# Two-block transformer kernel: closing norm in two token halves, second feed-forward norm with its root and tiles in PSUM, other banks for the first pairs of two stages

## Chip, cores, metric

One core of one Trainium2 chip. The metric is the device time of one execution in microseconds; three runs of the kernel before gave 1818.01, 1818.57 and 1822.48, median 1818.57.

## What is computed

Two transformer blocks over 512 tokens of width 1024, all in 32-bit floats, transposed (features on partitions, tokens on columns). The part that matters here:

```
x = x + rmsnorm(merged @ w_out[l], g_mix_post[l])        # out2, post2
h = rmsnorm(x, g_ffn_pre[l])                             # the norm of ffn2
gu = h @ w_ffn_in[l]                                     # ffn2, 44 units
f = (jax.nn.silu(gu[..., :D_FF_2]) * gu[..., D_FF_2:]) @ w_ffn_out[l]   # down2a, down2b
x = x + rmsnorm(f, g_ffn_post[l])                        # closing norm and store
```

with `rmsnorm(x, g) = x * rsqrt(mean(x * x) + eps) * g` over the features of a token. The first block has the same shape: out1, ffn1, down1a and down1b.

## The kernel before

**Weights.** All weight matrices are one stream of 278 units of 128 x 1024 (512 KB). A ring of three slots holds them: SP loads a unit into `w_raw` (L318), ScalarE rounds it to `w_hi` (L820, `feed`), GpSimd computes the rest `w_lo = w_raw - w_hi` (L335, `low_part`), and TensorE forms each product as three matmuls, hi x hi, hi x lo and lo x hi (`split_mm`, L378 to L380). A slot is filled again once `w_used` has counted the unit that was in it; `feed_after(t)` feeds unit t + 2. GpSimd's work is the ring, in the order of the units; `ring(0, FIRST["ffn2"] + AHEAD)` runs until two units of ffn2 are split, then come the seven sums of squares of ffn2's norm (L356), then the ring goes on.

**Stages.** Each stage multiplies a run of units with an activation tensor that is held as a hi and a lo part. `tiles_loop` runs out1, ffn1, out2 and ffn2: every unit gives 128 output features for 512 tokens, 24 matmuls of 512 columns in one PSUM bank, units alternating between banks 0 and 1. The first two units run together (`two_units`): k tile by k tile, as the lo parts of the input become ready, in banks 0 and 1. TensorE takes a bank with `acquire`, which waits for the reader's `bank_free`.

**Out2 to ffn2.** VectorE copies each unit of out2 to `o2` (L1773), ScalarE squares, VectorE sums (L1343), TensorE multiplies the sum with a matrix of ones (L514, `norm`; fp32, it stands in the trace as two records), ScalarE makes the root by Ln and Exp (L849, L851) in `tmp[3]`. Then `post` on VectorE, for each of eight tiles: scale by root and gain (L1793), add to `hT` (L1798), and the low part `u_lo` for ffn2 (L1372, `raw_low`); ScalarE squares (L845) and makes `u_hi` (L855); GpSimd sums the squares (L356). Ffn2 begins on the unnormed `u_hi`, `u_lo`; its root is applied to the outputs. Before the last k tile of the first two units TensorE runs the ones matmul. In `ffn_dve` VectorE handles a pair of units: gate times root (L1643), sigmoid on ScalarE (L1160), two products, the other unit (L1651), and the split of the result into `a_hi` (L1654) and `a_lo` (L1655). The gate's read frees bank 0 (L1644), the other bank 1.

**Down and close.** `down2a` and `down2b` accumulate eleven units each into four banks (2 to 5, then 6, 7, 0, 1); the last unit goes bank by bank. VectorE copies each bank to `o3` (L1809), the squares are summed, one ones matmul, one root, then `post` again: eight scales of 512 columns on VectorE (L1793), adds to `hT` alternately on VectorE (L1798) and GpSimd (L361), and eight stores of 256 KB by SP (L326). The file's helpers `step` and `wait_ge` order the engines by semaphores; nothing else plans the work.

Of the kernel before, what the change touches and what calls it, by code (L numbers as in the profile page):

```python
# [26 lines left out]
P = 128  # L27
# [87 lines left out]
def build(nc, stream, xT, memT, vecs, tabs, relb, outT):  # L115
    with ExitStack() as ctx, ExitStack() as work:
# [110 lines left out]
        sticks = [tmp[0], tmp[1], at("stick2", [P, T], F32, mv_at), at("stick3", [P, T], F32, mv_at + 2 * K)]  # L227
        zero_l = ar("zero_l", [P, P], BF16, 72)
# [7 lines left out]
        ps = ctx.enter_context(nc.psum_tensor("ps", [P, 8, T], F32))  # L236

# [28 lines left out]
        PER_NORM = {"sq": KT, "add": KT - 1, "ms": 1, "rs": 1}  # L266

        def of_norm(name, kind, value):

            if kind in PER_NORM:  # L270
                before_it = NORMS.index(name) * PER_NORM[kind]
            else:
                before_it = (SCALED if kind == "u" else SPLITS).index(name) * KT
            return named("norm_" + kind), before_it + value


# [16 lines left out]


# [7 lines left out]
        def _(sp):  # L302
# [24 lines left out]
            sp.wait_ge(out_done, 16 * KT)  # L327
# [3 lines left out]
        def _(pool):  # L331
# [18 lines left out]
            ring(0, FIRST["ffn2"] + AHEAD)  # L350

            for k in range(1, KT):
# [3 lines left out]
                pool.tensor_tensor(tmp[2][:, :], tmp[2][:, :], tmp[k % 2][:, :], ALU.add).then_inc(named("norm_add"), 1)  # L356
            ring(FIRST["ffn2"] + AHEAD, UNITS)

            for k in range(1, KT, 2):
                pool.wait_ge(named("y_out_scaled"), k + 1)  # L360
                pool.tensor_tensor(hT[:, k], hT[:, k], tmp[4 + k % 2][:, :], ALU.add).then_inc(named("y_odd"), 1)  # L361
# [3 lines left out]
        def _(pe):  # L365
# [26 lines left out]
            def two_units(t, xh, xl, n, ready, before_last=None):  # L392

                pe.wait_ge(lo_ready, t + 2)
                acquire(0)
                acquire(1)
                for k in range(KT):
                    if k == KT - 1 and before_last:
                        before_last()
                    pe.wait_ge(*(of_norm(*ready, k + 1) if isinstance(ready, tuple) else (ready, k + 1)))  # L400
                    c = slice(k * P, k * P + P)
                    for j in range(2):
                        slot = (t + j) % R
                        m = split_mm(ps[:, j, 0:n], w_hi[:, slot, c], w_lo[:, slot, c], xh[:, k], xl[:, k],
# [53 lines left out]
            def tiles_loop(name, n, xh, xl, ready, before_last=None):  # L458

                u, turn = FIRST[name], 2 * R  # L460
                two_units(u, xh, xl, T, ready, before_last)
                for j in range(2, turn):
                    tile_unit(u + j, (u + j) % R, j % 2, xh, xl)
# [58 lines left out]
            def softmax_attention(name, steps, head_q, head_k, keys, values, extra, out_of, opens, ready, between,  # L522
# [6 lines left out]
                for g in range(turns + 2):  # L529
                    if g < turns:  # L530

                        if g >= 1:
                            pe.wait_ge(named(name + scored), 2 * g)
# [5 lines left out]
                        for e in range(2):  # L539
# [5 lines left out]
                            m.then_inc(named(name + "_s"), 1)  # L545
                    if g >= 2:
# [5 lines left out]
                        pe.wait_ge(named(name + "_pt"), s + 2)  # L552
                        nb = keys[steps[s][1]] // P
                        two_heads = steps[s][0] != steps[s + 1][0]
                        for e, kb in sorted(product(range(2), range(nb)), key=lambda x: x[::-1] if two_heads else x):
# [4 lines left out]
                            if kb == nb - 1:  # L560
                                m.then_inc(named(name + "_av"), 1)
# [4 lines left out]
                    if 1 <= g <= turns:  # L566
                        if g == 1:
                            settle([4, 5])
                        for e in range(2):
                            s = 2 * (g - 1) + e  # L570

                            pe.wait_ge(named(name + "_pn"), s + 1)
# [3 lines left out]
                            m.then_inc(named(name + "_t"), 1)  # L576
# [89 lines left out]
            for j in range(8):  # L666
                if j == 1:
                    pe.wait_ge(named("moba_y"), 4)
                yh, yl = (yb_hi, yb_lo) if j % 2 == 0 else (ya_hi, ya_lo)
                up_unit(u + j, (u + j) % R, yh, yl, 2 * (j % 2))  # L670
            tiles_loop("out1", 8, m1_hi, m1_lo, ready=named("m1_lo_done"))
            tiles_loop("ffn1", 44, u_hi, u_lo, ("n_ffn", "lo"), lambda: norm("n_ffn", T))
# [113 lines left out]
            pe.wait_ge(named("dsa_y"), 4)  # L786
            pe.wait_ge(named("mem_y"), 4)
# [8 lines left out]
            tiles_loop("out2", 8, m2_hi, m2_lo, ready=named("m2_lo_done"))  # L796
            norm("n_post2", T)
            tiles_loop("ffn2", 44, u_hi, u_lo, ("n_ffn2", "lo"), lambda: norm("n_ffn2", T))
            down("down2a", [2, 3, 4, 5], named("ffn2_a"))
            down("down2b", [6, 7, 0, 1])  # L800
# [1173 lines left out]
```

## Time and profile before

| what | value |
|---|---|
| three runs | 1818.01, 1818.57, 1822.48 us |
| profiled execution, its own time | 1820.88 us |
| its span, first to last instruction | 1819.1 us |
| TensorE busy | 1726.2 us, 95% |
| VectorE, ScalarE, GpSimd busy | 869.7, 625.1, 704.9 us |
| mean granted TensorE clock | 0.987 of full speed |
| memory traffic | 162.21 MB moved, mean 89 GB/s |

The profile follows one execution. A busy share is an average over stages; what a change in a stage is worth is read from the waits of that stage. Times in a row of a timeline are counted from the start of the span, and a bracket at its end tells how long the engine had stood idle before it and which instruction released it.

### The profile page before, as it was taken

What the parts mean: (1) busy time and instruction counts of PE and PEld (TensorE: products, weight loads), DVE (VectorE), ACT (ScalarE), POOL (GpSimd) and SP (SyncE); (2) the same over time, 40 slices, a digit from 0 to 9 for tenths busy, and PEclk for the clock granted to TensorE, in tenths of its full rate; (3) what the DMA queues carried; (4) which work ended last, traced back from release to release, by engine and by line L of the source; (5) the groups of instructions that cost most, each with busy time, mean ns of one, the idle gap of its engine ahead of it and who ended that gap; (6) DMA issues with size and microseconds to landing.
All of it is one profiled execution on the core that took longest, in us unless ns stands there. A gap on an engine that the chain in (4) does not pass through costs nothing.

```text
span 1819.1 us, 23230 instructions
## 1 busy us (share of the span) xinstructions
PE 1726.2 (95%) x7880; PEld 1356.0 (75%) x7888; DVE 869.7 (48%) x1341; ACT 625.1 (34%) x997; POOL 704.9 (39%) x293
## 2 busy tenths in 40 slices
PE   5999999999999999998899899999999699999995
PEld 4888666777888887886578655668888488888884
DVE  6603665573655552035497756541332755555003
ACT  5233444434222223234424444453222422222221
POOL 2544222244544444444243111224444444444442
PEclk9999999999999999999999999999999899999998
DMA  4434311223322232234122111112332132232321
GB/s 154 160 130 117 103 58 47 69 72 115 113 94 92 94 103 93 93 104 151 61 93 74 43 36 35 59 45 95 94 102 93 36 115 92 92 103 94 103 93 46
DMA packets 46189, 162.21 MB, mean 89 GB/s; under 512 B 5564, under 2 KB 5692, under 8 KB 45864
## 3 DMA queue, kind: packets, MB, share of 16 engines
q1 hardware_dynamic: 42576, 151.16, 25.4%
q10 hardware_dynamic: 3544, 10.13, 1.7%
q8 instruction: 43, 0.70, 0.2%
q14 instruction: 26, 0.21, 0.0%
HBM read 156.91 MB, written 4.76 MB: 89 GB/s over the span
## 4 chain that ended last, share of the span: by engine, by line
PE 53%; issue 29%; POOL 10%; DVE 6%; ACT 2%; POOLq 0%; DVEq 0%; ACTq 0%
PE ps L378 16%; PE ps L380 16%; PE ps L379 16%; POOL w_lo L335 10%; PE ps L537 1%; PE ps L558 1%; DVE tmp L1343 1%; DVE tmp L1793 1%; PE ps L574 1%; PE ps L749 1%; DVE sum L1763 1%; PE ps L705 1%; DVE hT L1798 1%; PE ps L771 0%; PE ps L514 0%
## 5 line engine op out<-in xcount | busy, mean ns | idle before, releaser
L335 POOL TENSOR_TENSOR w_lo<-w_raw,w_hi 128x1024 fp32r<-128x1024 f32 x278 | 686.7, 2472 | 1068.4 <-ACT w_hi L820 1068.3
L378 PE MATMUL ps<-u_hi,w_hi 128*128 128x512 f32 x1392 | 565.1, 406 | 37.5 <-DVE u_lo L1355 11.6
L380 PE MATMUL ps<-u_hi,w_lo 128*128 128x512 f32 x1392 | 546.3, 392 | 0.0
L379 PE MATMUL ps<-u_lo,w_hi 128*128 128x512 f32 x1392 | 545.8, 392 | 0.0
L820 ACT ACTIVATE w_hi<-w_raw 128x1024 fp32r<-128x1024 f32 x278 | 292.7, 1055 | 425.5 <-PE ps L380 384.9
L378 PEld LDWEIGHTS ps<-u_hi,w_hi 128*128 128x128 f32 x1392 | 263.1, 189 | 117.0 <-issue 54.2
L380 PEld LDWEIGHTS ps<-u_hi,w_lo 128*128 128x128 f32 x1392 | 263.2, 189 | 56.4
L379 PEld LDWEIGHTS ps<-u_lo,w_hi 128*128 128x128 f32 x1392 | 263.6, 189 | 52.9 <-issue 2.4
L378 PE MATMUL ps<-a_hi,w_hi 128*128 (+1 forms) x352 | 137.2, 390 | 0.3 <-POOL w_lo L335 0.3
L380 PE MATMUL ps<-a_hi,w_lo 128*128 (+1 forms) x352 | 137.0, 389 | 0.0
L379 PE MATMUL ps<-a_lo,w_hi 128*128 (+1 forms) x352 | 137.0, 389 | 0.0
L1655 DVE TENSOR_TENSOR a_lo<-tmp,a_hi 128x512 f32 (+1 forms) x44 | 115.8, 2632 | 5.2
L1160 ACT ACTIVATE tmp<-tmp 128x512 f32<-128x512 f32 x44 | 27.8, 632 | 222.0 <-DVEq L1645 221.9
L1651 DVE TENSOR_TENSOR tmp<-ps,tmp 128x512 f32<-128x512 f32 x44 | 30.4, 692 | 100.5 <-PE ps L380 100.2
L378 PEld LDWEIGHTS ps<-a_hi,w_hi 128*128 128x128 f32 x352 | 66.1, 188 | 14.4 <-issue 0.8
L379 PEld LDWEIGHTS ps<-a_lo,w_hi 128*128 128x128 f32 x352 | 66.1, 188 | 13.8
L380 PEld LDWEIGHTS ps<-a_hi,w_lo 128*128 128x128 f32 x352 | 66.1, 188 | 13.7
L1643 DVE TENSOR_TENSOR tmp<-ps,tmp 128x512 f32<-128x512 f32 x44 | 30.4, 692 | 62.3 <-PE ps L380 49.5
L1809 DVE COPY o<-ps 128x512 f32<-128x512 f32 x8 | 5.5, 688 | 106.8 <-PE ps L380 106.8
L1613 DVE TENSOR_TENSOR tmp<-ps,tmp 128x512 f32<-128x512 f32 x16 | 11.1, 692 | 91.1 <-PE ps L380 90.0
L1679 DVE TENSOR_TENSOR hT<-ps,hT 128x512 f32<-128x512 f32 x8 | 5.5, 688 | 98.1 <-PE ps L380 98.1
L378 PE MATMUL ps<-m_hi,w_hi 128*128 128x512 f32 x128 | 50.0, 391 | 1.4 <-DVEq L1587 0.9
(279 smaller groups left out, 2160.7 us busy)
## 6 DMA issues: line engine op xcount, KB each, us to landing
w_raw<-stream SPq DMA_DIRECT2D x278, 512.0 KB, 3.5
g_rep<-g_one ACTq DMA_DIRECT2D x1, 2560.0 KB, 15.2
hT<-xT SPq DMA_DIRECT2D x4, 512.0 KB, 5.2
spread<-m_rows ACTq DMA_DIRECT2D x4, 512.0 KB, 4.6
tmp<-tmp ACTq DMA_DIRECT2D x32, 64.0 KB, 3.6
bias<-g_rep ACTq DMA_DIRECT2D x1, 2048.0 KB, 7.9
outT<-hT SPq DMA_DIRECT2D x8, 256.0 KB, 2.0
mem_in<-memT ACTq DMA_DIRECT2D x1, 1024.0 KB, 4.8
```

Source lines behind the costliest of these rows:

```text
L335: pool.tensor_tensor(w_lo[:, slot], w_raw[:, slot], w_hi[:, slot].bitcast(F32), ALU.subtract)\
L378: pe.matmul(out, wh, xh, start=start, stop=False)
L379: pe.matmul(out, wh, xl, start=False, stop=False)
L380: return pe.matmul(out, wl, xh, start=False, stop=stop)
L537: both.append(pe.matmul(ps[:, 2 + e, 0:keys[t]], head_q(h, t), head_k(h, keys[t]), start=True, stop=not extra(t)))
L558: m = pe.matmul(ps[p0:p1, b, t * P:t * P + P], values(h, kb), prT[e][:, kb * P:kb * P + P], start=kb == 0, stop=kb == nb - 1)
L574: m = pe.transpose(ps[:, 4 + e, kb * P:kb * P + P], pr[s % 4][:, kb * P:kb * P + P], ident)
L820: act.activation(w_hi[:, slot], w_raw[:, slot], ACT.Copy).then_inc(hi_ready, 1)
L1160: act.activation(tmp[0][:, :], tmp[1][:, :], ACT.Sigmoid).then_inc(named(name + "_e"), 1)
L1643: step(dve.tensor_tensor(tmp[1][:, :], ps[:, 0, :], tmp[3][:, :], ALU.mult))
L1651: step(dve.tensor_tensor(tmp[4][:, :], ps[:, 1, :], tmp[2][:, :], ALU.mult))
L1655: step(dve.tensor_tensor(a_lo[:, bass.ds(k, 1)], a, a_hi[:, bass.ds(k, 1)].bitcast(F32), ALU.subtract))
```

## The change

1. `out1` and `out2` run their first pair in banks 4 and 5, all others in 0 and 1 (`out_banks`). `ffn1` and `ffn2` run pairs 0 and 2 in banks 6 and 7, all others in 0 and 1 (`ffn_banks`).
2. Post2: the root goes to PSUM bank 3 (`post_rs`), the scaled tiles to banks 4 and 5 (`post_t`). The squares have five buffers; GpSimd sums the first six, and TensorE multiplies that sum and the last two squares with ones, three matmuls into one bank, before k tiles 6 and 7. The weight copy of ffn2's third unit stands before post2's root on ScalarE, its low part before the sums on GpSimd.
3. `down2b`: units 0 to 7 over all 512 tokens; units 8 to 10 for tokens 0 to 255 in banks 2 and 3, then for tokens 256 to 511 in the banks of before. Half 0's norm is formed while half 1 is multiplied. For half 1 ScalarE squares from PSUM and TensorE sums over four ones matmuls. Each half has its own root, scales, adds (VectorE and GpSimd in turn, the odd ones' scaled tiles in PSUM) and eight stores of 128 KB.
4. The three softmax attentions share their semaphores, with offsets (`of_attention`).

```diff
+        late_sq = ar("late_sq", [P, 4, HALF], F32, 88)
+        t_even = ar("t_even", [P, KT // 2, HALF], F32, 92)
+        LATE = [6, 7, 0, 1]
...
+        def late_out(n, half):
+
+            return ps[:, 2 + n // 2, HALF * (n % 2):HALF * (n % 2) + HALF] if half == 0 else ps[:, LATE[n], HALF:T]
+
+        late_rs = [ps[:, 5, 0:HALF], ps[:, 3, 0:HALF]]
+        late_rs_sbuf = tmp[5][:, 0:HALF]
+        LAST = [[0, 1, 2, 3, 4, 5, 6, 7], [4, 5, 6, 7, 0, 1, 2, 3]]
+        t_odd = [ps[:, 4, HALF:T], ps[:, 5, HALF:T]]
...
+        post_rs = ps[:, 3, :]
+        post_t = [ps[:, 4, :], ps[:, 5, :]]
+
+        def square_2(k):
+            return (tmp[0] if k == 0 else [tmp[1], tmp[2], tmp[4], tmp[5]][(k - 1) % 4])[:, :]
+
+        def out_banks(pair):
+
+            return (4, 5) if pair == 0 else (0, 1)
+
+        def ffn_banks(pair):
+
+            return (6, 7) if pair in (0, 2) else (0, 1)
...
-            for k in range(KT):
-                sp.wait_ge(named("y_odd" if k % 2 else "y_out"), k // 2 + 1)
-                sp.dma_start(outT[:, k], hT[:, k]).then_inc(out_done, 16)
+            for half in range(2):
+                cols = slice(HALF * half, HALF * half + HALF)
+                for i, k in enumerate(LAST[half]):
+                    sp.wait_ge(named("y_odd" if i % 2 else "y_even"), KT // 2 * half + i // 2 + 1)
+                    sp.dma_start(outT[:, k, cols], hT[:, k, cols]).then_inc(out_done, 16)
...
-            ring(0, FIRST["ffn2"] + AHEAD)
-
-            for k in range(1, KT):
+            ring(0, FIRST["ffn2"] + R)
+
+            for k in range(1, POOLED):
                 pool.wait_ge(*of_norm("n_ffn2", "sq", k + 1))
                 if k >= 2:
                     pool.wait_ge(*of_norm("n_ffn2", "add", k - 1))
-                pool.tensor_tensor(tmp[2][:, :], tmp[2][:, :], tmp[k % 2][:, :], ALU.add).then_inc(named("norm_add"), 1)
+                pool.tensor_tensor(square_2(0), square_2(0), square_2(k), ALU.add).then_inc(named("norm_add"), 1)
...
+                for i, k in enumerate(LAST[half]):
+                    if i % 2:
+                        continue
+                    pool.wait_ge(named("y_scaled"), KT * half + i + 1)
+                    pool.tensor_tensor(hT[:, k, cols], hT[:, k, cols], t_even[:, i // 2], ALU.add)\
+                        .then_inc(named("y_even"), 1)
...
+                if k == POOLED:
+                    acquire(2)
+                    pe.wait_ge(*of_norm("n_ffn2", "add", POOLED - 1))
+                    pe.matmul(ps[:, 2, :], ones, square_2(0), start=True, stop=False).then_inc(named("norm_ms"), 1)
+                if k == KT - 1:
+                    for last in range(POOLED, KT):
+                        pe.wait_ge(*of_norm("n_ffn2", "sq", last + 1))
+                        pe.matmul(ps[:, 2, :], ones, square_2(last), start=False, stop=last == KT - 1)\
+                          .then_inc(named("norm_ms"), 1)
...
+            acquire(2)
+            acquire(3)
+            for j in (8, 9, 10):
+                pe.wait_ge(lo_ready, u + j + 1)
+                for n, k2 in (sorted(product(range(4), range(2))) if j == 10 else
+                              [(n, k2) for k2 in range(2) for n in range(4)]):
+                    m = late_unit(j, (u + j) % R, fixed_a(j)(k2), n, k2, late_out(n, 0), 0, HALF,
+                                  j == 8 and k2 == 0 and n % 2 == 0, j == 10 and k2 == 1 and n % 2 == 1)
+                    if j == 10 and k2 == 1 and n % 2 == 1:
+                        m.then_inc(named("late_a"), 1)
+
+            pe.wait_ge(named("late_taken"), 4)
+            for j in (8, 9, 10):
+                for i, (n, k2) in enumerate(sorted(product(range(4), range(2))) if j == 10 else
+                                            [(n, k2) for k2 in range(2) for n in range(4)]):
+                    if j == 9 and i == 4:
+                        acquire(4)
+                        pe.wait_ge(*of_norm("n_fpost2", "add", 7))
+                        pe.matmul(ps[:, 4, 0:HALF], ones, tmp[2][:, 0:HALF], start=True, stop=True)\
+                          .then_inc(named("norm_ms"), 1)
+                        pe.matmul(ps[:, 2, 0:HALF], ones, tmp[2][:, HALF:T], start=True, stop=False)
+                    m = late_unit(j, (u + j) % R, fixed_a(j)(k2), n, k2, late_out(n, 1), HALF, T,
+                                  False, j == 10 and k2 == 1)
+                    if j == 10 and k2 == 1:
+                        m.then_inc(named("late_b"), 1)
+            for n in range(4):
+                pe.wait_ge(*of_norm("n_fpost2", "sq", 8 + n + 1))
+                m = pe.matmul(ps[:, 2, 0:HALF], ones, late_sq[:, n], start=False, stop=n == 3)
+            m.then_inc(named("norm_ms"), 1)
...
-            root("n_post2", T)
+            feed_after(FIRST["ffn2"])
+            root("n_post2", T, dst=post_rs)
...
+            late_root(0, 4)
+            for n in range(4):
+                act.wait_ge(named("late_b"), n + 1)
+                act.activation(late_sq[:, n], late_out(n, 1), ACT.Square).then_inc(named("norm_sq"), 1)
+            late_root(1, 2)
...
+            dve.wait_ge(*of_norm("n_post2", "rs", 1))
+            for k in range(KT + 2):
+                if k < KT:
+                    if k >= 2:
+                        dve.wait_ge(named("post2_x"), k - 1)
+                    dve.scalar_tensor_tensor(out=post_t[k % 2], in0=o2[:, k], scalar=v("post2", k), in1=post_rs,
+                                             op0=ALU.mult, op1=ALU.mult).then_inc(named("post2_x_scaled"), 1)
+                if 1 <= k <= KT:
+                    dve.wait_ge(named("post2_x_scaled"), k)
+                    dve.tensor_tensor(hT[:, k - 1], post_t[(k - 1) % 2], hT[:, k - 1], ALU.add)\
+                       .then_inc(named("post2_x"), 1)
+                if k >= 2:
+                    raw_low("n_ffn2", "ffn2", k - 2)
...
+            for half in range(2):
+                cols = slice(HALF * half, HALF * half + HALF)
+                dve.wait_ge(*of_norm("n_fpost2", "rs", half + 1))
+                for i in range(KT + 1):
+                    if i < KT:
+                        k = LAST[half][i]
+                        if half and k == 0:
+                            dve.wait_ge(*of_norm("n_fpost2", "rs", 3))
+                        o = late_out(k - 4, 1) if half and k >= 4 else o3[:, k, cols]
+                        rs = late_rs_sbuf if half and k >= 4 else late_rs[half]
...
+                        dve.scalar_tensor_tensor(out=t, in0=o, scalar=v("fpost2", k), in1=rs,
+                                                 op0=ALU.mult, op1=ALU.mult).then_inc(named("y_scaled"), 1)
+                    if i >= 2 and i % 2 == 0:
+                        k = LAST[half][i - 1]
+                        dve.wait_ge(named("y_scaled"), KT * half + i)
+                        dve.tensor_tensor(hT[:, k, cols], t_odd[(i - 1) // 2 % 2], hT[:, k, cols], ALU.add)\
+                           .then_inc(named("y_odd"), 1)
```

## Rows read from the trace of the kernel before

**Rows 1.** Windows view: stretch, length, busy (x count) per engine, clock, DMA, GB/s

```profile
1416.00:1449.30 33.30, 18.52 (x55) 10.95 (x53) 25.87 (x28) 15.33 (x23) 14.23 (x8) 0.80 0.05 17
1724.00:1797.50 73.50, 73.50 (x326) 60.71 (x324) 7.25 (x11) 15.35 (x17) 27.49 (x12) 1.00 0.20 64
1797.50:1819.10 21.60, 2.25 (x3) 0.50 (x2) 13.47 (x17) 2.58 (x4) 6.57 (x4) 0.58 0.26 97
```

**Rows 2.** Waits of TensorE, whole span: total us, times, longest

```profile
PE ps L378 <- DVEq L1644: 2.4, 2, 1.2
PE ps L378 <- DVEq L1627: 1.3, 2, 1.0
PE ps L378 <- DVEq L1587: 1.2, 2, 0.9
```

**Rows 3.** Timeline of TensorE, start of ffn2: start us, us, instruction, idle before

```profile
1426.92 0.76 PE L378 MATMUL ps<-u_hi,w_hi 128*128 128x512 f32 x1 [5.96 <-DVE u_lo L1372]
...
1432.79 0.50 PE L378 MATMUL ps<-u_hi,w_hi 128*128 128x512 f32 x1 [0.20 <-DVE u_lo L1372]
...
1445.43 0.39 PE L380 MATMUL ps<-u_hi,w_lo 128*128 128x512 f32 x1
...
1446.74 0.39 PE L379 MATMUL ps<-u_lo,w_hi 128*128 128x512 f32 x1
...
1449.27 0.47 PE L378 MATMUL ps<-u_hi,w_hi 128*128 128x512 f32 x1 [1.20 <-DVEq L1644]
```

**Rows 4.** Timeline of VectorE, post2 and the first pair of ffn2

```profile
1422.47 1.42 DVE L1793 SCALAR_TENSOR_TENSOR tmp<-o,vec,tmp 128x512 f32<-128x512 f32 x2 [3.69 <-ACT tmp L851]
...
1430.31 1.76 DVE L1798 TENSOR_TENSOR hT<-hT,tmp 128x512 f32<-128x512 f32 x1
...
1442.45 3.35 DVE L1372 SCALAR_TENSOR_TENSOR u_lo<-hT,vec,u_hi 128x512 fp32r<-128x512 f32 x2
...
1451.67 0.69 DVE L1651 TENSOR_TENSOR tmp<-ps,tmp 128x512 f32<-128x512 f32 x1
```

**Rows 5.** Timeline of GpSimd, same stretch

```profile
1429.80 1.72 POOL L356 TENSOR_TENSOR tmp<-tmp,tmp 128x512 f32<-128x512 f32 x1 [1.89 <-ACT tmp L845]
...
1451.13 5.22 POOL L335 TENSOR_TENSOR w_lo<-w_raw,w_hi 128x1024 fp32r<-128x1024 f32 x2 [3.07 <-ACT w_hi L820]
```

**Rows 6.** Timeline of SP, one issue, and the page's issues (KB each, us to landing)

```profile
1415.93 0.33 SPq L318 DMA_DIRECT2D w_raw<-stream  x1
...
w_raw<-stream SPq DMA_DIRECT2D x278, 512.0 KB, 3.5
...
outT<-hT SPq DMA_DIRECT2D x8, 256.0 KB, 2.0
```

**Rows 7.** Groups by form: busy us, mean ns; last row: min/median/max ns

```profile
L820 ACT ACTIVATE w_hi<-w_raw 128x1024 fp32r<-128x1024 f32 x278 | 292.7, 1055 | 425.5 <-PE ps L380 384.9 <-issue 20.2 <-DMA w_raw<-stream 8.6
L849 ACT ACTIVATE tmp<-ps,small 128x256 f32<-128x256 f32 x1 | 0.5, 474 | 0.5 <-PE ps L514 0.5
L851 ACT ACTIVATE tmp<-tmp 128x256 f32<-128x256 f32 x1 | 0.4, 417 | 0.1
L1355 DVE TENSOR_TENSOR um_lo<-tmp,um_hi 128x256 fp32r<-128x256 f32 x8 | 3.4, 425 | 0.2
L1361 DVE SCALAR_TENSOR_TENSOR tmp<-mem_in,vec,tmp x8: 472/484/1199, 687.8 to 693.4; 128x256 f32<-128x256 f32 x8
```

**Rows 8.** Timeline of TensorE in mk: first and 48th matmul of 256 columns

```profile
801.45 0.28 PE L378 MATMUL ps<-um_hi,w_hi 128*128 128x256 f32 x1
...
807.09 0.28 PE L380 MATMUL ps<-um_hi,w_lo 128*128 128x256 f32 x1
```

**Rows 9.** Timeline of the end: last matmul of down2b, first scale, last GpSimd add

```profile
1797.32 0.39 PE L380 MATMUL ps<-a_hi,w_lo 128*128 128x512 f32 x1
...
1804.70 1.42 DVE L1793 SCALAR_TENSOR_TENSOR tmp<-o,vec,tmp 128x512 f32<-128x512 f32 x2 [3.69 <-ACT tmp L851]
...
1814.99 1.64 POOL L361 TENSOR_TENSOR hT<-hT,tmp 128x512 f32<-128x512 f32 x1 [1.29 <-DVE tmp L1793]
```

More of the change, by code:

```diff
@@ L266, in build @@
         PER_NORM = {"sq": KT, "add": KT - 1, "ms": 1, "rs": 1}
+        POOLED = 6
+        OTHER_SUMS = {"n_ffn2": {"sq": KT, "add": POOLED - 1, "ms": 1 + KT - POOLED, "rs": 1}}
         def of_norm(name, kind, value):
             if kind in PER_NORM:
-                before_it = NORMS.index(name) * PER_NORM[kind]
+                before_it = sum(OTHER_SUMS.get(n, PER_NORM)[kind] for n in NORMS[:NORMS.index(name)])
             else:
@@ L274, in of_norm, with of_attention @@
             return named("norm_" + kind), before_it + value
+        def of_attention(name, kind, value):
+            steps, outputs = {"moba": (0, 0), "mem": (32, 4), "dsa": (48, 8)}[name]
+            return named("attention" + kind), (outputs if kind in ("_y", "_yhi") else steps) + value
         A_STEPS = [(2 * p + e, t) for p in range(NHA // 2) for t in range(QT) for e in range(2)]
@@ L355, in _ @@
                     pool.wait_ge(*of_norm("n_ffn2", "add", k - 1))
[L356 to L361 removed]
+                pool.tensor_tensor(square_2(0), square_2(0), square_2(k), ALU.add).then_inc(named("norm_add"), 1)
+            ring(FIRST["ffn2"] + R, UNITS)
+            for half in range(2):
[6 more added lines that the diff above has]
+                        .then_inc(named("y_even"), 1)
         @block.tensor
@@ new lines, in whole, with fixed_a @@
+            def whole(j, t, slot, a_of, first=False):
+                pe.wait_ge(lo_ready, t + 1)
+                for k2 in range(2):
+                    for n in range(4):
+                        if first and k2 == 0:
+                            acquire(LATE[n])
+                        m = late_unit(j, slot, a_of(k2), n, k2, ps[:, LATE[n], :], 0, T, first and k2 == 0, False)
+                m.then_inc(w_used, 1)
+            def fixed_a(j):
+                return lambda k2: lambda x: x[:, 2 * j + k2]
@@ new lines, in _, with moving_a @@
+            whole(0, u, u % R, fixed_a(0), first=True)
+            with pe.Fori(0, 2) as i:
+                for j in range(R):
+                    def moving_a(k2, j=j):
+                        return lambda x: x[:, bass.ds(i * (2 * R) + (2 * (1 + j) + k2), 1)].rearrange("p a n -> p (a n)")
+                    whole(1 + j, i * R + (u + 1 + j), (u + 1 + j) % R, moving_a)
+            whole(7, u + 7, (u + 7) % R, fixed_a(7))
+            acquire(2)
[8 more added lines that the diff above has]
+                        m.then_inc(named("late_a"), 1)
@@ L1658, in ffn_dve @@
                 turns = 44 // per
-                with repeat(dve, turns, [(own, 6 * R), (made, R)]) as i:
+                for j in range(R):
+                    pair(u + 2 * j, j, ffn_banks(j))
+                with repeat(dve, turns - 1, [(own, 6 * R), (made, R)]) as i:
                     for j in range(R):
-                        pair(i * per + (u + 2 * j), i * R + j)
+                        pair(i * per + (u + per + 2 * j), i * R + (R + j))
                 for j in range(turns * R, FT):
@@ new lines, in late_add @@
+            def late_add(n):
+                dve.wait_ge(*of_norm("n_fpost2", "sq", 4 + n + 1))
+                dve.wait_ge(*of_norm("n_fpost2", "add", 3 + n))
+                dve.tensor_tensor(tmp[2][:, 0:HALF], tmp[2][:, 0:HALF], tmp[n % 2][:, 0:HALF], ALU.add)\
+                   .then_inc(named("norm_add"), 1)
+            dve.wait_ge(named("late_taken"), 4)
+            for n in range(4):
+                dve.wait_ge(named("late_a"), 1 + n // 2)
+                x = o3[:, 4 + n, 0:HALF]
+                dve.tensor_tensor(x, late_out(n, 0), x, ALU.add).then_inc(named("n_fpost2_src"), 1)
+                if n >= 1:
+                    late_add(n - 1)
```

190 lines of the change are left out of this document (104 added, 86 removed).

## Prediction

> **What bounds the kernel now.** I read the page first (busy shares, the span in slices, the chain), then the stretches, the waits of TensorE, and the timelines around the waits. TensorE is what the time is made of: from 1724.0 to 1797.5 it is busy for all 73.5 us, 326 recorded matmuls of 512 columns, 0.227 us from start to start (326 x 0.227 = 74, a few records missing or cut at the edges) [rows 1]. So a microsecond taken from another engine counts only where TensorE stands. It stands in three kinds of places that the change touches. In 1416.0 to 1449.3, the way from out2 into ffn2, it works 18.5 of 33.3 us and its mean clock is 0.80; after 1797.5 it has 2.3 us of work in 21.6 us, at 0.58 [rows 1]. And it waits for banks that VectorE has yet to release: twice for L1644 (2.4 us in all, each 1.2: the third units of ffn1 and ffn2), twice for L1627 (1.3, the longest 1.0: the start of ffn1, so 0.3 for the third unit of out1), and for L1587 0.9 at the start of out1 [rows 2].
>
> **Part 1, banks.** With banks 4 and 5 for the first pair of out1 and out2, nothing at the start of out1 asks for bank 1, which L1587 frees: minus 0.9, and the third unit finds bank 0 free: minus 0.3. Out2's third unit I price like out1's, minus 0.3. Ffn1 starts on banks 6 and 7: minus 1.0; its third unit takes bank 0, free since out1: minus 1.2. Here something else is late next. The fourth unit's weights are split only after the sigmoid. In ffn2 that GpSimd turn begins at 1451.13 and takes 2.6 (two in 5.22) [rows 5], done at 1453.7; the third unit, freed from its wait, starts at 1449.27 - 1.2 = 1448.1 [rows 3] and ends 24 matmuls later, 24 x 0.227 = 5.4, at 1453.5. So 0.2 to 0.3 comes back. Ffn1 has the same shape: 1.0 + 1.2 - 0.3 = 1.9. Part 1 without ffn2: 0.9 + 0.3 + 0.3 + 1.9 = **3.4**. A bank named earlier costs nothing; cover is that the last use of banks 4 to 7 was stages before. Between here and the end the stages shift as they are.
>
> **Part 2, the second feed-forward norm.** The eight tiles of post2 take VectorE from 1422.47 to 1442.45 + 3.35 = 1445.80 [rows 4]. A tile is scale, add, low part: 0.71 + 0.69 + 0.74 alone. But at 1430.31 the add takes 1.76, and it ends 0.55 after the GpSimd sum that began at 1429.80 and took 1.72 [rows 4, 5]: a VectorE instruction with two SBUF inputs waits until GpSimd's has ended. At 1451.67, GpSimd busy from 1451.13 on, a product with one input in PSUM takes its plain 0.69 [rows 4, 5]. The change puts the root and the scaled tiles into PSUM, so that scale and add each have one SBUF input; only the low part keeps two, and its place right after the add is before GpSimd's next sum. I take 2.0 us a tile (2.14 less the overlap of neighbours), 1422.5 + 8 x 2.0 + 0.5 = 1439.0 for the last low part. Two sums of GpSimd go (seven to five).
>
> The Trainium skill, GPSIMD Engine Reference, section 1, says that GpSimd's SBUF interface is shared with VectorE instructions of two SBUF inputs, which is what the rows show. Against the change speaks VectorE: DVE Perf Modes, section on the TRN2 errata: a fixed part of 58 cycles at 0.96 GHz with an SBUF source, 120 with one in PSUM, so 0.065 us more per moved instruction, an estimate of 1.0 us for the sixteen here and 0.8 for the twelve that end the kernel; by it the result would be 0.8 later. The 0.69 above bears no such part, so the sum leaves it out.
>
> Then TensorE is the later one. First low part: its first matmul was at 1426.92 [rows 3]; I keep 1426.8. Two tiles of six matmuls ran at the half clock, until 1432.79 with a small wait [rows 3]; now 1432.0. A ones matmul costs 1446.74 - 1445.43 less two plain pitches of 0.23, so 0.85 [rows 3]; three stand where one stood (six squares summed, two raw ones). So 1432.0 + 4 tiles x 1.37 + 0.3 of small waits + 0.85 + 1.37 + 1.7 + 1.37 = 1443.1 for the start of the third unit, against 1449.27: minus 6.2. The weight chain again: last ones matmul out at 1441.8; before it was out at 1446.7, and the fourth unit's low part was done at 1453.7, 7.0 later; so 1448.8, while the third unit ends at 1448.5: plus 0.3. Net **5.9**, bank wait included. The moved weight copy: the raw unit is asked for at 1415.93 and lands 3.5 later, 1419.4 [rows 6]; its copy takes 1.06 [rows 7] and is done at 1420.5, before the root begins at about 1421.0. GpSimd then splits it before the sums, where it was idle; SP's next load comes earlier. Cost nothing; if the load came 2 us late, root and all behind it would slip by 1.5.
>
> **Part 3, the closing norm by halves.** The last three units (72 matmuls of 512, 16.3 us) become 144 of 256 columns. In mk such matmuls stand from 801.45 to 807.09, 47 steps, 0.120 each [rows 8]: 17.3 us, plus 1.0. Two ones matmuls of 256 columns stand among them: plus 0.85. The last matmul starts at 1797.32 + 1.85 = 1799.2 [rows 9] and is out at 1799.4. All of half 0 lies beside TensorE's work: units 0 to 7 end at 1781.2, half 0's columns at 1789.9, the copies, sums and squares on VectorE and ScalarE need about 3.5 us and TensorE asks for them at 1794.2; root at 1795.8, VectorE's twelve instructions until 1800.8. Late next if that cover goes: half 1, ready for VectorE at 1801.9.
>
> After the last matmul: square 0.42, ones matmul 0.43, Ln 0.47, Exp 0.42 [rows 7], the ones matmul half the one of 512 columns [rows 3], and 0.8 of handing over: 2.5, where it was 1804.70 - 1797.7 = 7.0 [rows 9]. Then eight scales and four adds of 256 columns at 0.48 and 0.43, starts some 0.08 closer [rows 7]: 8 x 0.40 + 4 x 0.35 + 0.3 = 4.9, GpSimd's fourth add ending beside. Before it was 1814.99 + 1.64 - 1804.70 = 11.9 [rows 9]. The store behind took 1819.1 - 1816.6 = 2.5 (landing 2.0 [rows 6]); sixteen stores of half the size, each issued as its half tile is done, I leave at that. So 1799.4 + 2.5 + 4.9 + 2.5 = 1809.3: minus **9.8**. The shared attention semaphores change names and offsets, no wait: nothing, as each stage's waits keep their order.
>
> Sum: 3.4 + 5.9 + 9.8 = 19.1. The profiled execution took 1820.9 with a span of 1819.1, 2.3 above the median of 1818.6; from 1820.9 I get 1801.8, on the median's footing **1799.5**.
>
> **Unknown prices.** No row shows VectorE writing PSUM, ScalarE's root into PSUM, or a read and a write in one bank. Below: 0.05 less than the plain row each, 0.6 for twelve. Above: 0.69 for 256 columns instead of 0.43, as if the fixed part doubled. I take the plain rows, since the PSUM source was plain. In part 2 TensorE hides up to 2.8 us of this. The clock could rise one tile sooner or later: 6 x 0.2 = 1.2. A smaller store: 0.5 either way.
>
> **Rivals.** (a) GpSimd still holds VectorE in post2: the low part stays at 1445.8 less two sums (1.7), TensorE two ones matmuls and two tiles behind; part 2 gives 1.5, time 1803.9. For: every low part has two SBUF inputs. Against: 1451.67. 0.09. (b) PSUM instructions at 0.69 in the closing: half 0 needs 8.3 and ends at 1804.1, after half 1 is ready (plus 2.2), half 1 3.4 longer: 1805.1. 0.09. (c) The halves do not pay: the weight load of 128 columns takes 0.19 and sets the pitch: 144 x 0.07 = 10 more, 1809.5. Against: [rows 8], where it overlapped. 0.03. (d) The other side: the 256-column matmuls, alternating two halves and banks, run one after the other at their recorded length of 0.28 or, at the half clock, more: 144 x 0.163 = 23.5, 1823; over a pitch of (1824.0 - 1799.5)/144 + 0.12 = 0.29 it is slower by over 0.3%. For: the record's length. Against: the starts in mk. 0.02. (e) More than forecast, with the clock rising early and the stores shorter: 1796, 0.07. The rest, 0.70, is the forecast, with its own range of 1796.5 to 1803.
>
> 0.3% (5.5 us) is about what a measurement here can tell from no change. Only (d) comes near it: half of it and a little of unknown causes stays within, 0.02 slower. Range 1795 to 1807: forecast, (a), (b), (e).
>
> **What would show it.** Right: no wait of TensorE for banks at the starts of out1, ffn1, and the third units; post2's adds at 0.69 throughout with PSUM names; ffn2's third unit some 27 us after out2's last matmul instead of 33; 256-column matmuls at 0.12; under 10.5 us from the last data matmul to the end. Wrong: post2 tiles at 3 us, a VectorE wait for `late_b` or roots in half 0, TensorE idle between unit 10's halves, or scale instructions over 0.6 at 256 columns.

## Result and profile after

The kernel after takes **1802.01 us** (median of 4 runs, 1801.3 to 1804.89) against 1818.29 (4 runs, 1817.62 to 1822.48): ratio 0.9909, 95% interval 0.9897 to 0.9922. Forecast were 1799.5 us and 1795 to 1807. The profiled execution took 1801.3 us with a span of 1799.5, 0.7 below its median; the one of before, 1820.88, lay 2.6 above its own (2.3 above the median of three runs that the prediction had). So the two spans differ by 19.6 us, and the medians by 16.3. Both numbers matter below.

The windows view for the three stretches that answer to [rows 1] (stretch, length, busy and count of PE, PEld, DVE, ACT and POOL, clock, DMA share, GB/s):

```profile
1412.00:1439.00 27.00, 18.62 (x58) 12.61 (x58) 17.82 (x27) 13.90 (x22) 8.81 (x6) 0.75 0.13 39
1716.20:1789.70 73.50, 73.50 (x394) 63.88 (x393) 12.87 (x29) 17.66 (x24) 28.71 (x15) 1.00 0.22 70
1789.70:1799.50 9.80, 1.82 (x9) 1.25 (x7) 5.60 (x15) 1.55 (x4) 3.51 (x5) 0.86 0.53 174
```

The way from out2's last matmul to ffn2's third unit is 27.0 us long where it was 33.3, with about the same TensorE work in it (18.6 us for 18.5): 6.3 us of standing still are gone, and VectorE's busy time fell from 25.9 to 17.8. Behind the last data matmul 21.6 us became 9.8. In the middle TensorE is as full as before.

What is left in the waits of TensorE (total us, times, longest):

```profile
PE ps L419 <- POOL w_lo L371: 4.0, 5, 2.8
...
PE ps L419 <- DVEq L1723: 0.3, 1, 0.3
```

No wait for a bank is left at the start of any of the four stages. The second line is another one: it stands at 380.8, in the stage ahead of out1, and before had it too, as 0.3 of the 1.2 that [rows 2] give for L1587. So 4.6 of the 4.9 us of [rows 2] are gone, and with them 0.25 for L1774 at out2's third unit. The first line is the weight chain that the prediction named as late next: 0.2 at ffn1's start, 0.3 at ffn1's fourth unit and 0.3 at ffn2's. (The rest, 0.35 in down1a and 2.8 in mk, is in stages whose length did not change: mk takes 15.95 us in both kernels.) Here is ffn2's, in the timeline of all engines, with GpSimd's pair of low parts:

```profile
1422.63 0.77 PE L419 MATMUL ps<-u_hi,w_hi 128*128 128x512 f32 x1 [5.69 <-DVE u_lo L1508]
...
1433.64 1.02 PE L847 MATMUL ps<-tmp,kept 128*128 128x512 f32 x2
...
1435.88 1.88 PE L851 MATMUL ps<-tmp,kept 128*128 128x512 f32 x4
...
1438.98 0.40 PE L419 MATMUL ps<-u_hi,w_hi 128*128 128x512 f32 x1
...
1442.21 5.22 POOL L371 TENSOR_TENSOR w_lo<-w_raw,w_hi 128x1024 fp32r<-128x1024 f32 x2 [10.67 <-ACT w_hi L933]
...
1444.94 0.50 PE L419 MATMUL ps<-u_hi,w_hi 128*128 128x512 f32 x1 [0.33 <-POOL w_lo L371]
```

The third unit stands at 1438.98 without a wait, 16.4 us behind the first matmul; it was 22.3 [rows 3]. One fp32 ones matmul is a pair of records (x2): the first, of GpSimd's sum, and the two of the raw squares (x4).

VectorE and GpSimd in post2 (the timeline of all engines), which answer to [rows 4, 5]:

```profile
1430.09 0.74 DVE L1925 SCALAR_TENSOR_TENSOR ps<-o,vec,ps 128x512 f32<-128x512 f32 x1
1430.24 1.30 POOL L392 TENSOR_TENSOR tmp<-tmp,tmp 128x512 f32<-128x512 f32 x1 [0.62 <-ACT tmp L1435]
...
1430.75 0.68 DVE L1929 TENSOR_TENSOR hT<-ps,hT 128x512 f32<-128x512 f32 x1
1431.35 0.74 DVE L1508 SCALAR_TENSOR_TENSOR u_lo<-hT,vec,u_hi 128x512 fp32r<-128x512 f32 x1
```

The add at 1430.75 runs in 0.68 inside GpSimd's 1430.24 to 1431.54; in before such an add took 1.76. GpSimd's own sum fell from 1.72 to 1.30. A tile takes 1.92. The low part keeps both its sources in SBUF. It begins 0.19 before the sum ends and ends 0.55 behind it, which is its plain 0.74.

The end, from the last data matmul on (timeline, all engines):

```profile
1789.50 0.28 PE L864 MATMUL ps<-a_hi,w_lo 128*128 128x256 f32 x1
1789.62 1.89 PE L913 MATMUL ps<-late_sq,kept 128*128 128x256 f32 x8
...
1790.27 0.42 DVE L1987 TENSOR_TENSOR hT<-ps,hT 128x256 f32<-128x256 f32 x1
...
1792.38 0.37 ACT L1456 ACTIVATE ps<-tmp 128x256 f32<-128x256 f32 x1
1792.51 0.48 DVE L1982 SCALAR_TENSOR_TENSOR t_even<-ps,vec,tmp 128x256 f32<-128x256 f32 x1 [1.82 <-ACT tmp L1455]
...
1796.08 0.73 POOL L401 TENSOR_TENSOR hT<-hT,t_even 128x256 f32<-128x256 f32 x1 [0.39 <-DVE t_even L1982]
...
1796.76 0.42 DVE L1987 TENSOR_TENSOR hT<-ps,hT 128x256 f32<-128x256 f32 x1
```

Half 0 was through VectorE at 1790.69 (the add at 1790.27), 1.8 us before half 1's first scale. Half 1 needs 3.0 us from the last matmul's start to the first scale, 4.7 in VectorE, 2.3 for the store: 10.0, where 21.8 stood [rows 9].

### The profile page after: what moved, and what is told of

Read it like the earlier page. It is cut to its first block, busy times and chain, and to the rows that moved or that the text cites. A ratio compares the mean times of both kernels' runs of the same rounds, so it can differ in the third digit from the quotient of the medians.

```text
span 1799.5 us, 23353 instructions
## 1 busy us (share of the span) xinstructions
PE 1730.3 (96%) x7974; PEld 1363.7 (76%) x7974; DVE 863.2 (48%) x1357; ACT 626.1 (35%) x1004; POOL 699.6 (39%) x295
## 4 chain that ended last, share of the span: by engine, by line
PE 54%; issue 30%; POOL 10%; DVE 4%; ACT 2%; POOLq 0%; ACTq 0%; DVEq 0%
PE ps L419 15%; PE ps L421 15%; PE ps L420 15%; POOL w_lo L371 10%; PE ps L863 1%; PE ps L862 1%; PE ps L864 1%; PE ps L580 1%; PE ps L601 1%; PE ps L792 1%; PE ps L617 1%; PE ps L748 1%; DVE tmp L1479 0%; PE ps L814 0%; PE ps L796 0%
## 5 line engine op out<-in xcount | busy, mean ns | idle before, releaser
L419 PE MATMUL ps<-a_hi,w_hi 128*128 (+1 forms) x264 | 102.9, 390 | 0.3 <-POOL w_lo L371 0.3
L420 PE MATMUL ps<-a_lo,w_hi 128*128 (+1 forms) x264 | 102.7, 389 | 0.0
L421 PE MATMUL ps<-a_hi,w_lo 128*128 (+1 forms) x264 | 102.7, 389 | 0.0
L419 PEld LDWEIGHTS ps<-a_hi,w_hi 128*128 128x128 f32 x264 | 49.6, 188 | 11.1 <-issue 0.8
L421 PEld LDWEIGHTS ps<-a_hi,w_lo 128*128 128x128 f32 x264 | 49.5, 188 | 10.3
L420 PEld LDWEIGHTS ps<-a_lo,w_hi 128*128 128x128 f32 x264 | 49.6, 188 | 10.2
L419 PE MATMUL ps<-w_hi,u_hi 128*128 128x512 f32 x128 | 50.4, 394 | 0.8 <-ACTq L998 0.8
```

The lines of the kernel that those rows point to most:

```text
L419: pe.matmul(out, wh, xh, start=start, stop=False)
L420: pe.matmul(out, wh, xl, start=False, stop=False)
L421: return pe.matmul(out, wl, xh, start=False, stop=stop)
```

## Experiments

Only stages that the change touches should differ. So I cut each profile into stages, by the start of GpSimd's low part of each stage's third unit, and set the touched ones apart from the rest of the span. The six touched stages, in four groups, and the rest, in us:

| profile | out1 | ffn1 | out2 + ffn2 | down2a + down2b + close | rest | time, median of runs |
|---|---|---|---|---|---|---|
| before | 47.2 | 247.2 | 305.8 | 139.8 | 1079.1 | 1818.3 |
| e0, before again | 47.2 | 247.2 | 305.8 | 139.8 | 1077.3 | 1818.9 |
| e1, banks alone | 45.6 | 246.0 | 303.6 | 138.9 | 1080.5 | 1816.7 |
| e2, second norm alone | 47.2 | 247.4 | 299.8 | 138.9 | 1077.6 | 1814.2 |
| e3, close alone | 47.2 | 247.4 | 304.7 | 130.0 | 1078.5 | 1810.7 |
| u1, after without the banks | 47.2 | 247.4 | 299.8 | 130.0 | 1078.1 | 1804.2 |
| after | 45.6 | 245.9 | 299.6 | 130.0 | 1078.4 | 1802.0 |
| a0, after again | 45.6 | 246.0 | 299.6 | 130.0 | 1080.9 | 1803.2 |

**e0 and a0, the two kernels again**, unchanged, for the scatter of one profile.

> The kernel before once more, with its own profile. Two theories of why the timed gain is 16.3 us and not the 19.1 of the sum. Theory A: the three edits give 19 us in every execution, and the profiled execution of before carried some 2 to 3 us of half-clock stretches in stages that the change leaves alone; then this profile shows the same waits at out1, ffn1, ffn2 and the close, its time is 1818 +- 1, and its half-clock stretches outside the changed stages sum to less than in the first profile of before. Theory B: one of the three edits gives less in most executions than in the profiled pair; then this profile shows a changed stage (1416 to 1449, or after 1797) shorter by 2 us or more than in the first profile. Ratio 1.000.

> The changed kernel once more. So far: the stage table of two profiles of before, of the three single edits and of the changed kernel agrees within 0.1 us in every stage that an edit leaves alone, except where a stretch at half clock falls (gate1a, cq, aq, ak, out2 and the last ones matmul). Theory A (the edits give 18 to 19 us stage by stage, and the timed 16.3 is scatter of those stretches from execution to execution): with more executions the median lies at 1800 to 1801.5, 17.5 to 19 below before. Theory B (timed executions hold something that the profiled ones do not): it stays at 1802 or above. The stage table of this profile: out1 45.6, ffn1 245.9, out2 and ffn2 together 298.5 to 299.6, down2b and the close 68.5.

Measured: 1818.92 us (12 runs, ratio 1.0007 [0.9998, 1.0015]) and 1803.16 (5 runs, 0.9905 [0.9889, 0.9921]). The touched stages repeat within 0.1 us, so a stage length shows small effects that a run's time does not. The rest moves by 1.8 and 2.5 us between two profiles of one program. It does so in few places: the stages aq, ak, cq, gif and gate1a, in which TensorE has pauses; all but gif also had short stretches at half clock in one profile or another. Aq was 60.4 us in one profile of before and 57.2 in the other, with the same code: the first has two such stretches in aq, the second one. E0's theory A also expected less half clock outside the touched stages than in the first profile; it was more, 20.5 us against 17.1, with a shorter rest. So the sum of such stretches does not tell the time, where they fall does. And a0's median lies where its theory B had it, at 1802 or above. The sum of the touched stages falls by 18.9 to 19.0 us from before to after.

**e1, the banks alone.**

```
-            tiles_loop("out1", 8, m1_hi, m1_lo, ready=named("m1_lo_done"))
+            tiles_loop("out1", 8, m1_hi, m1_lo, ready=named("m1_lo_done"), banks=out_banks)
...
+                for j in range(R):
+                    pair(u + 2 * j, j, ffn_banks(j))
```

> Before, with only the banks of the first pairs changed (out1, out2, ffn1, ffn2). Theory A (the sum): out1 0.9 + 0.3, out2 0.3, ffn1 1.9, ffn2 1.2 less 0.3: minus 4.3 us, 1814.0. Theory B, if banks are the part that gives less: minus 1.5 to 2. In the trace the waits for L1587, L1627, L1644 and L1774 are gone, and TensorE waits 0.2 to 0.3 us for the low part of the fourth unit.

**e2, the second feed-forward norm alone** (with the semaphores shared among the attentions, as in after).

```
-            return (4, 5) if pair == 0 else (0, 1)
+            return (0, 1)
...
-            return (6, 7) if pair in (0, 2) else (0, 1)
+            return (0, 1)
...
+                sp.dma_start(outT[:, k], hT[:, k]).then_inc(out_done, 16)
```

The diff is against the kernel after; the closing norm is that of before.

> Before, with only post2 changed: root and scaled tiles in PSUM, six squares summed by GpSimd and three ones matmuls, the weight copy of the third unit moved ahead of the root; first pairs in banks 0 and 1. Theory A: the third unit still waits about 1.2 us for bank 0, so the gain is 5.9 less 0.9: minus 5.0 us, 1813.3. Theory B, if this is the part that gives less: minus 2 to 3. VectorE's adds stand at 0.69 throughout, tiles 2.0 apart.

**e3, the closing norm by halves alone**, against the kernel after, with both bank functions as in e2.

```
-        OTHER_SUMS = {"n_ffn2": {"sq": KT, "add": POOLED - 1, "ms": 1 + KT - POOLED, "rs": 1}}
+        OTHER_SUMS = {}
...
-            tiles_loop("ffn2", 44, u_hi, u_lo, ("n_ffn2", "lo"), before_each=mean_square_2, banks=ffn_banks)
+            tiles_loop("ffn2", 44, u_hi, u_lo, ("n_ffn2", "lo"), before_last=lambda: norm("n_ffn2", T), banks=ffn_banks)
```

> Before, with only the closing norm in two halves. Theory A: minus 9.8 us, 1808.5. Theory B, if the close is the part that gives less: minus 7. The 256-column matmuls stand 0.12 apart, VectorE's instructions of 256 columns take 0.48 and 0.42, from the last data matmul to the end 10 us.

Measured: e1 1816.7 us (0.9991 [0.9982, 0.9999]), e2 1814.21 (0.9975 [0.9965, 0.9985]), e3 1810.71 (0.9959 [0.9946, 0.9972]). In the stages each part does its own and little else (ffn1 is 247.4 for 247.2 in e2, e3 and u1, in which, as in after, VectorE handles the first three pairs of ffn1 and ffn2 ahead of its loop). Out1 and ffn1 are shorter by 1.6 and 1.3 with the banks; the closing stage is 8.9 shorter in e3 than in e1 and e2, 9.9 than in before. Ffn2 needs care: at its start TensorE's half-clock stretch was 13.7 us long in before and after, and 10.2 in e1, e2 and e3. The longer one begins before post2's own ones matmul, which then takes 2.0 us and not 1.1. E3, with the code of before there, is 1.1 us shorter than before: that is the price in the old norm. In the new one it is 0.95: ffn2's first matmul stands 10.8 us behind out2's last one in after, and 9.9 in e2 and u1. Against e3, the banks give 1.1 in ffn2 and the second norm 4.9. Timed, the three give 2.2, 4.7 and 8.2 us against the runs beside them, 15.1 together.

**u1, the kernel after without the banks**: `out_banks` and `ffn_banks` return (0, 1) always, as in e2.

> The kernel after without the other banks: the first units of out1, out2, ffn1 and ffn2 all use banks 0 and 1 again, the other two parts stay. From the stages of the kernel with the banks alone, out1 should be 1.6 us longer (47.2), ffn1 1.3 (247.2), and in ffn2, where the third unit still waits for the gate and the norm, about 1.1; 4.0 in all. The timed loss should be the same if the parts add up (1807 against 1802.5). Rival: in the kernel after, ffn2's start is set by the tiles of post2 and by the half clock, so the banks are worth nothing there, and the loss is 2.9; and if less than 2 is timed, the gain of the parts in whole runs is smaller than in the profiled stages.

Measured: 1804.23 us (0.9916 [0.9903, 0.9929]), 2.2 and 1.1 us above the medians of after and a0. The stages: out1 47.2 and ffn1 247.4, as expected; out2 + ffn2 299.8, only 0.2 above after, but with the 10.2 us stretch, so 1.15 at equal clock. So the banks are worth 3.0 us in out1 and ffn1 by the stages and 1.15 in out2 and ffn2, and whole runs show 1.1 to 2.2. In the rest, e1 and u1 part as well: 1080.5 with the banks, 1078.1 without.

**p1, post2's root and scaled tiles in SBUF**, all else as in after.

```
-        post_rs = ps[:, 3, :]
-        post_t = [ps[:, 4, :], ps[:, 5, :]]
+        post_rs = tmp[3][:, :]
+        post_tiles = ar("post_tiles", [P, 2, T], F32, 64)
+        post_t = [post_tiles[:, 0], post_tiles[:, 1]]
```

> The changed kernel with post2's root and scaled tiles back in SBUF (root in tmp[3], tiles in a free place), all else as changed. If PSUM names are what keeps GpSimd's sums from holding VectorE (my reading of the hold), scales and adds take 1.3 to 1.7 where a sum runs, tiles stand 2.6 to 3.0 apart, the last low part comes 4 to 7 us later and the third unit of ffn2 2 to 4 us later: 1805. Rival: fewer sums and better order do it, PSUM nothing: tiles 2.0 apart, 1802.

Measured: 1807.16 us (0.9932 [0.9917, 0.9946]), 4.0 above a0, which ran beside it; ffn2 259.6 us against 254.8, and it had the shorter half-clock stretch, so 5.7 at equal clock. The timeline of all engines:

```profile
1428.48 0.74 DVE L1926 SCALAR_TENSOR_TENSOR post_tiles<-o,vec,tmp 128x512 f32<-128x512 f32 x1
...
1428.63 1.73 POOL L393 TENSOR_TENSOR tmp<-tmp,tmp 128x512 f32<-128x512 f32 x1 [1.29 <-ACT tmp L1436]
1429.14 1.77 DVE L1930 TENSOR_TENSOR hT<-post_tiles,hT 128x512 f32<-128x512 f32 x1
```

The sum runs from 1428.63 to 1430.36. The scale had begun 0.15 before it and takes its plain 0.74; it is GpSimd that is late. The add that comes during the sum ends at 1430.91, 0.55 behind it. Each of the five tiles with a sum pays 1.1 us this way, and takes 3.0; ffn2's third unit comes 5.5 us later than in after. The fewer sums alone do not give the gain; the PSUM addresses do. With the tiles in SBUF, out2 + ffn2 take 304.4 us against 303.6 in e1, which has the same banks and the same stretch: the rest of the second norm's edit (fewer sums, three ones matmuls, the moved weights) costs 0.8 by itself.

**p2, GpSimd sums all eight squares.**

```
-        POOLED = 6
+        POOLED = 8
```

with one ones matmul, of the sum, in the place of three.

> The kernel after, in which GpSimd sums all eight squares of the second feed-forward norm and TensorE's ones matmul reads that one sum. Two squares' ones matmuls (1.88 us for both in the trace of the kernel after) leave TensorE. GpSimd gets two sums more of 1.29; the last would end 1.3 us after the last square, at about 1437.3 on the time scale of the profile of the kernel after's copy, where TensorE reaches the ones matmul at 1438.46. If the sums are covered, the stage from the start of ffn2 is 1.7 to 1.9 us shorter (252.9 against 254.8 us) and the time 1.7 shorter. Rival: the two sums run beside the last two low parts on VectorE; if GpSimd held those as it held the adds with both sources in SBUF (1.76 in place of 0.68), they end a us later each, TensorE waits for them, and nothing is gained (254.5 or more). The trace with post2's tiles in SBUF speaks against that: there a scale of 0.74 ran at 0.74 beside a sum.

Measured: 1800.73 us (0.9898 [0.9883, 0.9914]); ffn2 253.6 us, 1.2 shorter, so between the two expectations. The timeline of all engines:

```profile
1432.70 2.98 POOL L392 TENSOR_TENSOR tmp<-tmp,tmp 128x512 f32<-128x512 f32 x2 [0.63 <-ACT tmp L1435]
1433.27 2.96 DVE L1508 SCALAR_TENSOR_TENSOR u_lo<-hT,vec,u_hi 128x512 fp32r<-128x512 f32 x2
...
1434.60 0.50 PE L419 MATMUL ps<-u_hi,w_hi 128*128 128x512 f32 x1 [0.25 <-DVE u_lo L1508]
```

The last two low parts take 1.48 each: behind the last scale nothing spaces them, they begin during GpSimd's sums, and the hold comes back. I had read "a scale of 0.74 beside a sum" in p1 as freedom of that kind of instruction. It was only first. TensorE waits a quarter microsecond for it at one tile; the third unit still comes 1.2 us earlier.

**p3, the weight feed at its old place**: the ring of GpSimd and ScalarE's `feed_after(FIRST["ffn2"])` behind the eight tiles again.

> The kernel after, with its weight feed ahead of the second feed-forward norm put back where the kernel before has it: ScalarE takes the high part of one more unit after the eight tiles and not before the root, and GpSimd its low part after its sums. The prediction gave this move 0.3 us at most (a short wait for weights that comes back at the fourth unit). If that is right the stage from the start of ffn2 is within 0.5 us of 254.8. Rival: the low part of 2.6 us then stands between GpSimd's sums and the low part of the next unit, which ends later by up to 2.6, and the wait of TensorE at the fourth unit grows from 0.3 to about 2.9; the stage would be some 257.

Measured: 1801.45 us (0.9899 [0.9885, 0.9912]); out2 + ffn2 298.8 us with the 10.2 us stretch, against 299.6 with the long one: 0.1 longer at equal clock. The low part of the moved unit ran in GpSimd's gap, and the wait at the fourth unit was again 0.34. The move is worth 0.1 us, which is the scatter of a stage.

**b1, TensorE kept busy around post2's root**, with nine ones matmuls whose result nobody reads.

```
+            keep_warm(3)
             norm("n_post2", T)
+            keep_warm(6)
```

> The changed kernel with nine ones matmuls on constant data into the unused bank 7 while TensorE waits around post2's ones matmul (three before, six behind it), results unused. If the half clock at the start of ffn2 costs what its rows say (a ones matmul 2.06 instead of 0.9, two tiles at 2.56 instead of 1.4), post2's root comes 1.0 earlier and TensorE follows the low parts with a tile of 1.4 in 1.92: the third unit 2.5 to 3.5 us earlier, 1799. Rival: the weights of the fourth unit, or the low parts, are as late: under 1 us. No stretch at half clock between out2 and ffn2, and less scatter from run to run.

Measured: 1803.56 us (0.9915 [0.9901, 0.9928]), nothing gained against a0; the stage is as its rival had it, under 1 us. The windows view from out2's last matmul to ffn2's third unit:

```profile
1412.40:1438.50 26.10, 24.17 (x76) 13.45 (x76) 17.84 (x27) 13.36 (x21) 9.28 (x7) 1.00 0.12 40
```

The clock is 1.00 (2.4 GHz) all the way, where it was 0.75. The stage is 0.9 us shorter, and all of it lies ahead of ffn2's first matmul, where post2's own ones matmul runs at full clock. From ffn2's first matmul to the third unit it is 16.4 us in both. So two tiles of six matmuls at 1.2 GHz cost nothing in after: at full clock a tile takes 1.4 us, VectorE's low parts come every 1.92, and TensorE waits 0.2 to 0.3 for each from the second tile to the sixth in b1. In after it has caught up with them by 1432.14.

**b3, b1 with the unsummed squares in fp32r**, and an fp32r copy of the ones. This changes the rounding of six squares' sums.

```
-            pe.matmul(ps[:, 2, 0:HALF], ones, late_sq[:, n], start=False, stop=n == 3)
+            pe.matmul(ps[:, 2, 0:HALF], ones_hi[:, :], late_sq[:, n], start=False, stop=n == 3)
```

> b1_warm, and the squares that go to TensorE unsummed (two in ffn2's norm, four in the closing one) are written rounded, as fp32r, so that their ones matmuls pass once instead of several times. The four closing ones matmuls took 1.9 us together behind the last data matmul; one of 256 columns would take 0.12 instead of 0.43: the root comes 0.9 earlier. In ffn2 two of 512 columns take 0.23 instead of 0.85: 1.2 earlier. Together 2 us below b1_warm. Rival: ScalarE's last square sets the end, gain under 0.5 in the close.

Measured: 1800.74 us (0.9899 [0.9884, 0.9915]). Ffn2 is 1.0 us shorter than in b1, not the 1.2 expected, and the closing stage 0.9 (67.65 against 68.52), for the ones matmuls at the end:

```profile
1789.39 1.02 PE L921 MATMUL ps<-late_sq,ones_hi 128*128 128x256 f32 x4
```

**b4, all three together**: b1, p2's sum of eight, and the late squares in fp32r.

> The kernel after with three edits together: nine ones matmuls that only keep TensorE busy around the root of post2 (in a bank that nobody reads then), GpSimd summing all eight squares of the second feed-forward norm, and the four late squares of the closing norm in fp32r with an fp32r copy of the ones (this changes the rounding of those sums). From the two earlier runs the first gave 0.9 us in the stage from the start of ffn2 and the last about 0.9 in the close; the sum of eight should give what it gives alone. If all add up: 254.8 - 0.9 - 1.8 = 252.1 us for the stage, 67.6 for the last, and 3.6 us less than the kernel after in time, 1798.7. Rival: with TensorE at full clock through the tiles it reaches the ones matmul earlier than GpSimd's last sum (about 1437.3), so that the sum of eight is no longer covered, and only half of the 1.8 comes.

Measured: 1799.53 us (5 runs, 1795.25 to 1800.44; 0.9886 [0.9871, 0.9900]), the lowest time of the study, though its interval overlaps that of after. Ffn2 253.0 us, the close 67.65. They do not add up: the sum of eight gives 0.9 us beside b1, where it gave 1.2 in p2. That is the number of its rival, but not its reason: the last sum ends at 1436.09, 0.4 before the ones matmul at 1436.49. The 0.3 are lost behind it. ScalarE's Exp of the root begins 0.41 us behind its Ln, for 0.11 in p2, and TensorE waits 0.6 us for weights at the fourth unit, for 0.3. B3 has both as well. These are the two kernels in which ScalarE also makes the fp32r copy of the ones; why its Exp comes late is not shown.

## Why the prediction was right, step by step

**Part 1** was forecast at 3.4. Out1 and ffn1 came 2.9 us shorter (1.6 and 1.3). Ffn1 is the term that was too large, 1.9 against 1.3, and out1 the one too small, 1.2 against 1.6 (the cut between the two is made by GpSimd, so a little may have changed sides). In ffn1 the waits for banks went, but a wait for weights of 0.2 came back at its start too, not only the 0.3 at the fourth unit. And the ones matmul at its end waits 2.0 us for VectorE's sum and not 1.6; it does so in e2, e3 and u1 too, which have none of the banks.

**Part 2**, forecast 5.9 and 0.3 for out2, measured 6.2. The tiles came at 1.92 us for the 2.0 taken, and the way from ffn2's first matmul to the third unit was 16.35 us for the 16.3 worked out (1426.8 to 1443.1). The 0.3 of weights came as 0.33. One reason in it was wrong without harm: I let the half clock set the pace of the first two tiles, and b1 shows that it does not. The moved weight copy was priced at nothing, and p3 agrees.

**Part 3**, forecast 9.8, measured 9.9 against before and 8.9 against e1 and e2, whose closing ones matmul took 1.1 us and not 2.0. So 0.9 of the 9.8 came from where a half-clock stretch fell in the profile that the forecast was read from. The pitch of 0.12 held, and the last matmul came 1.9 us later in its stage, for 1.85. From there to the end it took 10.0 us for the 10.1 forecast. Inside, the handing over was 0.3 longer, VectorE's part and the store 0.2 shorter each.

**Rivals.** (a) is out: p1 makes it happen on purpose, and costs 4.0 us timed and 5.7 in the stage at equal clock. (b) is out: with PSUM the scale takes 0.48 and the add 0.41 at 256 columns, as the SBUF rows [rows 7] had it. The Trainium skill, VectorE: DVE Perf Modes, section on the TRN2 errata, would make each 0.065 us dearer; no row here shows that, at 256 columns or at 512 (0.74 and 0.68). (c) and (d) are out by the 0.12, and (e), 1796, did not come. The Trainium skill, GPSIMD Engine Reference, section 1, says that the SBUF interfaces of GpSimd are shared with VectorE, with contention when a VectorE instruction has two SBUF inputs: p1 and p2 agree, with 1.77 and 1.48 where two sources are in SBUF and a sum is running.

**The sum** was 19.1, and the touched stages give 18.9. Taken to the median it should have been 1799.5, and it was 1802.0: the runs give 16.3 and not 19. The number lies in the range; that it lies 2.5 above the forecast is not explained by any of the three parts. Three things on record bear on it.

First, the gap is not the banks'. E2 and e3 have none, and they fall short too: by the table 6.7 and 10.7 us less than before in the touched stages, timed 4.7 and 8.2. U1 falls short by 1.3, e1 by 3.7, after and a0 by 2.6 and 3.0. Every changed kernel does; what they share is the comparison with before.

Second, the two profiles of before may show more in the touched stages than most of its executions have. Both had the longer half-clock stretch in ffn2 (1.1 us) and the closing ones matmul at 2.0 us (0.9). E1 and e2, with the same code at the close, had 1.1 us for it. Without these 2.0 us the touched stages of before would be 738.0, and e2, e3, u1 and after would come out at 4.7, 8.7, 13.6 and 16.9 less for 4.7, 8.2, 14.3 and 16.3 timed; e1 would still lack 1.7. This fits, but it is argued: before was profiled twice, and no timed execution tells where its half clock fell.

Third, the rest of the span scatters by as much as is sought. It is 1078.1 us on average in the five profiles without the banks (1077.3 to 1079.1) and 1080.1 in the nine with them (1078.4 to 1082.2), and the 2.0 between them are mostly aq (1.2), gif (0.35) and down1a (0.3). But gif lies ahead of everything that the banks change, and aq goes by something else: in seven profiles its first half-clock stretch begins between 1040 and 1043 and it takes 60.4 to 60.8 us, in six between 1025 and 1028 and it takes 59.3, and e0, with one stretch only, has 57.2. After and a0, one program, stand in different groups. No run here moved the stages by a delay alone. What takes the 2.5 us stays open.

## What to carry to other kernels

Where VectorE and GpSimd work side by side, look at which VectorE instructions have two sources in SBUF and begin during a GpSimd instruction: here they ended half a microsecond after it. Putting the intermediate into a free PSUM bank removed that, and scales and adds took no longer for it (0.74 and 0.68 us). When a final norm can be split by tokens, the first half can lie under TensorE's last matmuls: here TensorE's own work grew by 1.9 us, and what was left after it fell from 21.8 to 10.0. And compare stages of two profiles before whole times: the touched stages repeated within 0.1 us here, and whole runs of one kernel spread over 2 to 9. Look also at what the two profiles have in half-clock stretches: 2 us of this kernel's forecast may have been that.

## What was not expected of the hardware

The hold between GpSimd and VectorE goes by who begins first: a scale that began 0.15 us before the sum took its plain 0.74, and GpSimd's sum then took 1.73 in place of 1.30 (p1). A mean clock of 0.75 over 27 us cost only 0.9 us, in post2's own ones matmul; in the tiles behind it VectorE set the pace (b1). ScalarE's root written to PSUM took 0.37 us, 0.05 less than the one written to SBUF. And untouched stages moved: one of 60 us by up to 3.6 between executions of like code, by where its half-clock stretches fell.
